# Feed-forward as one sequence with one ring of weight pieces: output parts of 6, 6, 6 chunks by seven products, 4 by eight, block sums on VectorE

## The reference, cut to what matters

```python
def swiglu(x, w_in, w_out):
    gate, up = jnp.split(x @ w_in, 2, axis=-1)
    return (jax.nn.silu(gate) * up) @ w_out

x = x + 0.5 * swiglu(rms_norm(x, ffn1_norm), ffn1_w_in, ffn1_w_out)
# mixers: attention, gated recurrence, short convolution
x = x + 0.5 * swiglu(rms_norm(x, ffn2_norm), ffn2_w_in, ffn2_w_out)
```

## Time and profile before

| | us |
|---|---|
| median of 3 runs | 2883.03 |
| lowest and highest run | 2880.31, 2888.37 |
| profiled execution, its own time | 2886.48 |
| span of the profiled execution | 2884.8 |
| TensorE matmuls busy | 2829.6 |
| VectorE busy | 1693.6 |
| ScalarE busy | 1112.6 |
| GpSimd busy | 312.8 |

### The profile page before, as it was taken

The page is one execution under the profiler, slowest core; times in us unless marked ns, Lnnn a source line. Parts: engine busy times, 40 slices in busy tenths (PEclk is TensorE's granted clock), DMA queues, the critical chain, the costliest instruction groups (busy, mean ns, idle before and its releaser), DMA issues.

```text
span 2884.8 us, 56179 instructions
## 1 busy us (share of the span) xinstructions
PE 2829.6 (98%) x21280; PEld 2764.3 (96%) x21280; DVE 1693.6 (59%) x2441; ACT 1112.6 (39%) x1669; POOL 312.8 (11%) x232
## 2 busy tenths in 40 slices
PE   7999999999999999999999999999999999999999
PEld 6999999899999999999999999998889999999998
DVE  4564756676655446656556565576666445575654
ACT  4332423555522333333333333335554223333324
POOL 1121201000000111111102021100000001030301
PEclk9999999999999999999999999999999999999999
DMA  3222223333222222222222223233332222222222
GB/s 121 73 88 87 88 74 99 90 96 87 82 80 87 89 85 70 95 73 97 80 76 87 88 73 103 74 89 90 90 107 71 87 80 97 74 81 95 73 88 91
DMA packets 299060, 249.22 MB, mean 86 GB/s; under 512 B 20643, under 2 KB 296307, under 8 KB 298919
## 3 DMA queue, kind: packets, MB, share of 16 engines
q1 hardware_dynamic: 296775, 242.44, 27.2%
q0 software_dynamic: 2144, 4.98, 0.5%
HBM read 240.04 MB, written 7.34 MB: 86 GB/s over the span
## 4 chain that ended last, share of the span: by engine, by line
PE 93%; DVE 3%; issue 1%; ACT 1%; DVEq 1%; DMA 0%; POOLq 0%; ACTq 0%; SPq 0%
PE ps L509 74%; PE ps L549 11%; PE ps L709 1%; PE ps L648 1%; PE ps L647 1%; PE ps L649 1%; PE ps L774 1%; PE ps L727 1%; PE ps L689 1%; DVE bl L1258 1%; DVE tmp L1223 1%; DVE wlo L1249 1%; PE ps L696 0%; PE ps L711 0%; DMA xin<-in_x_sample 0%
## 5 line engine op out<-in xcount | busy, mean ns | idle before, releaser
L509 PE MATMUL ps<-hh,whi 128*128 128x288 f32 x4480 | 965.3, 297 | 11.5 <-DVE wlo L1217 5.0
L509 PE MATMUL ps<-hl,whi 128*128 128x288 f32 x4480 | 959.3, 296 | 0.0
L509 PE MATMUL ps<-hh,wlo 128*128 128x288 f32 x4480 | 959.2, 296 | 0.0
L873 ACT ACTIVATE whi<-wraw 128x1024 fp32r<-128x1024 f32 (+1 forms) x388 | 403.9, 1042 | 1162.5 <-PE ps L509 1136.0
L509 PEld LDWEIGHTS ps<-hh,whi 128*128 128x128 f32 x4480 | 722.0, 189 | 14.2 <-DVE wlo L1217 5.9
L509 PEld LDWEIGHTS ps<-hh,wlo 128*128 128x128 f32 x4480 | 722.1, 189 | 0.0
L509 PEld LDWEIGHTS ps<-hl,whi 128*128 128x128 f32 x4480 | 721.9, 189 | 0.0
L1217 DVE TENSOR_TENSOR wlo<-wraw,whi 128x1024 fp32r<-128x1024 f32 (+1 forms) x388 | 467.0, 1204 | 374.4 <-ACT whi L873 373.6
L1266 DVE TENSOR_TENSOR tmp<-tmp,ps 128x576 f32<-128x576 f32 x128 | 96.6, 754 | 344.9 <-PE ps L509 344.5
L549 PE MATMUL ps<-bh,whi 128*128 128x288 f32 x896 | 266.8, 298 | 18.3 <-ACT tmp L956 12.8
L549 PE MATMUL ps<-bl,whi 128*128 128x288 f32 x896 | 264.3, 295 | 0.0
(11 more groups left out here) (333 smaller groups left out, 3549.9 us busy)
## 6 DMA issues: line engine op xcount, KB each, us to landing
wraw<-in_ffn_w_in SPq DMA_DIRECT2D x88, 1024.0 KB
wraw<-in_ffn_w_out SPq DMA_DIRECT2D x32, 1024.0 KB
wraw<-in_w_in SPq DMA_DIRECT2D x28, 1024.0 KB
wraw<-in_w_in SPq DMA_DIRECT2D x56, 512.0 KB
wraw<-in_ffn_w_out SPq DMA_DIRECT2D x16, 768.0 KB
wraw<-in_w_branch SPq DMA_DIRECT2D x24, 512.0 KB
wraw<-in_w_out SPq DMA_DIRECT2D x9, 1024.0 KB
kv<-in_cache_k SPq DMA_DIRECT2D x128, 64.0 KB, 1.8
```

The costliest lines, as they stand in the source:

```text
L509: last = pe.matmul(ps[slot][:, half, 0:HF], weights, rhs[:, k, half * HF:(half + 1) * HF], start=(start and c == 0 and n == 0), stop=(stop ...
L873: act.activation(split_tile(into, j, rowwise), raw_tile(slot, j, rowwise), ACT.Copy).then_inc(hi_ready, 1)
```

## The change

**One sequence.** A network is now one stage of 38 units, written out without loops: for each of 11 steps an up unit and then a gate unit (`whole`), four output units ahead of the gate unit of steps 3, 6 and 9, and four last output units. Parts one to three have 6 hidden chunks each, by seven products; the last part has 4, by eight. The gates and ups stay plain products.

**One ring.** Every tile, plain ones too, now passes through the ring of four as pieces: two of 512 columns for a gate or up tile, seven of 384 for an output unit, two of 256 for a last tile. After piece i, ScalarE and VectorE split piece i + 4.

**Sums on VectorE.** `weight_sums` leaves GpSimd. VectorE makes the sum for piece i + 6 after its split of piece i + 4, with a drain ahead of it, in three buffers in place of four.

**Moved.** The decay constants go from the preamble into the first network of each layer, behind the gate of step 4. `past_forgets` goes ahead of the last gate unit's load and waits for the third output part. The hidden blocks' last operations stand in the up unit that follows.

```diff
+STEPS = 11
+PART_STEPS = ((0, 1, 2), (3, 4, 5), (6, 7, 8), (9, 10))
+LAST = 9
+def ffn_units():
+    units = []
+    for s in range(STEPS):
+        units.append(("up", s, 0))
+        if s in (3, 6, 9):
+            units += [("out", s // 3 - 1, v) for v in range(4)]
+        units.append(("whole", s, 0))
+    return units + [("last", 3, v) for v in range(4)]
...
-        for pairs in (4, 4, 3):
-            s[name].append((Stage(plan, pairs, 2, 4), Stage(plan, 2, 2, 4), 2 * pairs))
+        s[name] = Stage(plan, 1, len(FFN_UNITS), 2 * len(FFN_UNITS))
...
-            bh = sb("bh", [P, 7, 4, HF], F32R, m)
-            wsum = sb("wsum", [P, 4, 4 * P], F32, m)
+                bh = sb("bh", [P, 7, 3, HF], F32R, m2)
+                wsum = sb("wsum", [P, 3, 4 * P], F32, m2)
...
             def ffn(name, L):
...
+                for n, (kind, s, v) in enumerate(FFN_UNITS):
+                    if kind == "up":
+                        load(S[name], n, L, 0, (w1, 0, KD, s * 256 + FFN, 256))
+                        if name == "ffn1" and s == STEPS - 1:
+                            past_forgets(L)
...
             def past_forgets(L):
-                norm = S["ffn1norm"]
-                wait_apart(sp, filled[norm.slot(0)], norm.turn(0, L) + 1)
+                st, k = S["ffn1"], 2 * FFN_UNITS.index(("out", 2, 3))
+                wait_apart(sp, filled[st.slot(k)], st.turn(k, L) + 1)
...
+            def ffn(name, nn, L):
+                st, f = S[name], nn // 2
+                root(S[name + "norm"], L)
+                i = 0
+                for n, (kind, s, v) in enumerate(FFN_UNITS):
+                    for m in range(7 if n in SEVEN_NO else 4):
+                        wait_done(act, st, f, i, L)
+                        if n in SEVEN_NO and m in (0, 1, 2, 4):
+                            parts(st, f, n, m, L)
+                        for j in BEHIND[i]:
+                            ring_split(st, f, j, L)
+                        if kind == "whole" and m % 2:
+                            if m == 3 and s < LAST:
+                                moving_first(f, s, s % 3, L)
...
+                            act.activation(buf, buf, ACT.Silu).then_inc(silu_ready, 1)
...
+            def weight_sum(st, f, i, L, first=None):
...
+                dve.drain()
...
+                dve.tensor_tensor(summed(n, m), x0, x1, op).then_inc(wsum_ready, 1)
...
+                        for j in BEHIND[i]:
+                            if j == 4:
+                                weight_sum(st, f, j + 1, L, first=i)
+                            ring_split(st, f, j, L)
+                            if j + 2 < len(ITEMS):
+                                weight_sum(st, f, j + 2, L)
...
+                        elif kind == "whole" and m == 3:
+                            if f == 0 and s == 4:
+                                dve.drain()
+                                decays()
+                            if s == STEPS - 1:
+                                odd_hidden(f, s, L)
...
-                for part in range(2):
-                    weight_sums(S["ffn1"][part][1], part_no(0, part), L)
```

More of the change, by code:

```diff
@@ L204, in build @@
             cmask = sb("cmask", [P, 2 * P], F32, m)
[L205 removed]
         with ExitStack() as m:
+            sb("over_th", [P, 8, 4 * HF], F32, m)
             yout = sb("yout", [P, 5, D], F32, m)
@@ new lines, in ring_ready, with seven @@
+            def ring_ready(st, f, i, L):
+                if COMB[i] is not None:
+                    pe.wait_ge(comb_lo, comb(L, f, i))
+                else:
+                    pe.wait_ge(lo_ready, st.unit(0, L) * 2 + (2 * ITEMS[i][0] + 2 + AHEAD))
+            def seven(st, f, n, i, L):
+                kind, s, v = FFN_UNITS[n]
+                first, second = ps[st.slot(2 * n)], ps[st.slot(2 * n + 1)]
+                a, b, c = first[:, 0, 0:HF], first[:, 1, 0:HF], second[:, 0, 0:HF]
+                half = chunks_of(n) // 2
+                for m, bank in enumerate((a, c, a, c, a, b, a)):
+                    ring_ready(st, f, i + m, L)
+                    if m < 2:
+                        wait_psum(st, 2 * n + m, L)
+                    if m in COPY_NO:
+                        pe.wait_ge(part_copied, copied(L, f, n, COPY_NO[m]))
+                    wh, wl = ring(whi, i + m), ring(wlo, i + m)
+                    x_ = MOVING[m]
+                    for kk in range(half):
+                        if v == 0:
+                            pe.wait_ge(mov_ready, blocks_ready(L, f, PART_STEPS[s][kk], MOVED[x_]))
+                        mov_h, mov_l = bh[:, x_, kk, :], bl[:, x_, kk, :]
+                        for t, (weights, moving) in enumerate(((wh, mov_h), (wh, mov_l), (wl, mov_h))):
+                            last = pe.matmul(bank, weights[:, kk, :], moving, start=(m in (0, 1, 5) and kk == 0 and t == 0),
+                                             stop=(m in (3, 5, 6) and kk == half - 1 and t == 2), skip_group_check=True)
+                    if m == 3:
+                        last.then_inc(filled[st.slot(2 * n + 1)], 1)
+                    elif m == 6:
+                        last.then_inc(filled[st.slot(2 * n)], 1)
+                    else:
+                        last.then_inc(product_done, 1)
@@ L970, in ffn, with buffers_free @@
[L970 to L990 removed]
+            def buffers_free(st, f, n, m, L):
+                kind, s, v = FFN_UNITS[n]
+                if kind == "out" and v == 0 and m == 0:
+                    act.wait_ge(mov_ready, blocks_ready(L, f, PART_STEPS[s][-1], 4))
@@ new lines, in parts @@
+            def parts(st, f, n, m, L):
+                kind, s, v = FFN_UNITS[n]
+                first, second = ps[st.slot(2 * n)], ps[st.slot(2 * n + 1)]
+                one, other = scratch(v)
+                places, scale = (one[:, 0:HF], other[:, HF:N], one[:, HF:N], None, other[:, 0:HF]), 0.5
+                buffers_free(st, f, n, m, L)
+                src = second[:, 0, 0:HF] if m == 1 else first[:, 0, 0:HF]
+                act.activation(places[m], src, ACT.Copy, scale=scale).then_inc(part_copied, 1)
@@ L1719, in _ @@
                     merge_step(i, False)
-                update(S["out"], L, 1.0, 16, L, 16)
+                update(S["out"], L, 16, L, 16)
                 dve.wait_ge(f_stored, L * 96 + 96)
@@ L1794, in _ @@
                 add_squares(L * 24 + 16)
-                for part in range(2):
-                    weight_sums(S["ffn2"][part][1], part_no(2, part), L)
                 add_squares(L * 24 + 24)
```

619 lines of the change are left out of this document (304 added, 315 removed).

## The result

The changed kernel takes 2901.1 us (median), the kernel before 2883.5 us beside it: a ratio of 1.0058, interval 1.0042 to 1.0074. One of its five runs took 11150.4 us, in the slow state, and is not in the ratio. The change makes the kernel slower by 0.58%, beyond the 0.3% that can be told apart, and 1 us above the upper end of the predicted range; the forecast was 2878. The profiled execution took 2901.01 us where the one before took 2886.48: 14.5 us more, where the sum of the prediction said 4.6 less. So 19.1 us have to be found.

What follows compares the result with a forecast made beforehand. TensorE, busy 98% of the span, was taken as the bound; -32.1 us removed and +27.5 added gave -4.6 net, so 2886.5 became 2882 profiled, 2878 as median, range 2858 to 2900.

Steps and rivals of the forecast that it cites:

- (a): Output parts by seven products, the last by eight: 948 products a network instead of 960, 48 fewer in all, -6.4 us.
- (b): The eight transitions where seven-product output units begin, two per network: TensorE's waits there all go, -21.2 us.
- The rival that the transitions stay: Waits move to the first unit of each output part, twelve parts cost 16 us, time 2894; chance 0.04.
- (c): At the four starts of a network TensorE goes on sooner, after one half split: -4.5 us, bounds -3 and -5.
- (d): Weight-block sums move from GpSimd to VectorE in the output units, so TensorE waits: +16 us, from 0 to 35.
- the loop: ScalarE and VectorE work in turn from one fourth sum to the next in output units: 8.73 us against TensorE's 8.45.
- binds harder: VectorE's in-order work between fourth sums at 36 output units costs up to 35 us, time 2897; chance 0.18.
- The Trainium skill's rule on drains: Next VectorE operation waits for an empty pipe: 9.4 us an output unit, about 38 us in all, result 2900.
- (e): At the gates' end, silu precedes the last hidden chunk; TensorE waits four times: +7 us, bounds 6 and 9.
- (f): TensorE waits once for every half piece, some 11 ns a wait: +3 us, bounds 0 and 4.
- (g): Past forgets' sixteen small loads on SyncE's queue hold the load behind them: +1.5 us for two layers, bounds 0 and 6.

Runs made afterwards that it cites:

- the second experiment: VectorE's drain and two additions of scratch to x moved from behind product five to behind product six, against the changed kernel: 2893.9 us, 1.0025 to the kernel before.
- the tenth experiment: On the kernel with the separate edits together, a network's last unit puts the addition to x and norm's cast ahead of the next stage's first split: 2867.2 us, 0.9929.

## Why the prediction was wrong

(a) **Right.** 48 fewer products; 3024 by seven, as the 1008 rows times three say.

(b) **Right, a little small.** The eight parts before lost 22.9 us beyond their products, where I took 21.2, and without the sums the new parts lose nothing. The rival that the transitions stay is out.

(c) **Right.** Behind the first tile the gates up to the first part now take 0.2 us more than their products, where they took 3.2, 0.7, 2.1 and 0.7 more: 6.0 against my 4.5.

(d) **Mechanism partly right, size too small**: 25.2 us, not 16. The forecast waits came where they were forecast, at the fourth product of the second to fourth unit of each part. By the starts each costs 0.47 us with the product behind it, 17 us in all for my 16; ScalarE's copy is ready there (248.07 in the second unit) just before VectorE's split (248.23). What I had left out are waits at the third product of the same units: 0.47, 0.11 and 0.19 us, together 9 us over the twelve parts. At the first of them, 246.69 above, TensorE waits for VectorE's split of the third piece, which stands behind the update of x:

```profile
245.64 0.45 DVE L1436 TENSOR_TENSOR x<-x,tmp 128x288 f32<-128x288 f32 x1
246.01 0.55 DVE L1344 TENSOR_TENSOR wlo<-wsum,whi 128x384 fp32r<-128x384 f32 x1
```

With the update late these waits are gone. Two terms of the loop were short too. The step from a split to the first sum takes 0.65 to 0.73 us, not 0.63: in the longer ones 0.17 is idle behind the drain. From ScalarE's split for the fourth sum to VectorE's last split it takes 2.05, not 1.88. That it is the loop alone fell with the second experiment: VectorE's own total, which I put at 8.66 and which by my prices is 8.50 without the drain that this edit saves, is 8.79 there. The point from which the "binds harder" rival decides was 9.1 us a unit; 9.03 was nearly there, and that rival had a chance of 0.18. The Trainium skill's rule on drains ("VectorE: DVE Perf Modes", section "The DRAIN you can't avoid"), by which I gave 9.4 us a unit and 2900 us, came near the measured time, but not for its reason. The section itself adds that a next operation that is not held starts earlier, and the trace agrees: undrained neighbours still start 0.47 us apart where each lasts 0.56. What a drain costs shows at the fourth sum: it starts 0.64 us after the split ahead of it with a drain between, 0.47 in the run without.

(e) **The wait right, the sentence behind it wrong.** Silu ahead of the last hidden chunk costs 1.6 us a network, 6.4 in all, against 7. The step that failed is the sentence with which I closed the term, "Behind it on VectorE stand only splits that TensorE needs later". That stage had not been stepped through. In it the pieces had become half pieces, the parts smaller and the chunks closer (3.2 us for 4.8), and the norm's chain had not; and each second split stood under GpSimd's addition. That is 1.5 us a network inside the stage, and it makes the last chunk late, whatever comes next: 3.1 us more before the transposes and 2.6 for their half clock, and 1.2 us at each of the two ways from the first feed-forward to the values. With the squares on VectorE the 1.5, the 1.2 and the half clock are gone, and the final wait is 1.8 us instead of 4.3. I had the contention in a row and used it only to say that it would go with the sums; GpSimd had one more job.

(f) **Wrong.** Half pieces with a wait each cost nothing: 576 plain products with a wait each 24 take 76.79 us, the last stage's 192 with a wait each 12 take 25.59 in the run with the tiles in turn, both 133.3 ns a product, and the parts without sums 133.0 ns with a wait each 9. The 0.9 ns in the old output stage belonged to that stage.

(g) **Right in kind and nearly in size.** 2.4 us for two layers, against 1.5.

**Open.** Why TensorE stands 2 to 4 us at the layer's turn before the third network, in every version with the new sequence. It stood there nearly as long in the kernel before:

```profile
1453.98 0.52 PE L509 MATMUL ps<-hh,whi 128*128 128x288 f32 x2 [1.80 <-issue]
```

So of the 2.1 us now only 0.3 can come from the change. The last stage's loss is not shown to be the cause either: without it the stop is longer, 3.9 us, and the tenth experiment moved the suspected work and not the stop. And which stop brings half clock: see below.

## What to carry to other kernels

When pieces are cut smaller, step through every stage that uses them, the shortest above all: a chain that ran once per piece now has less time for each, and each engine's order in it decides. Before a move off GpSimd is counted as the end of its contention, list what GpSimd still does, and what small VectorE operation stands in its way: the small one can pay the length of the large one, here 1.62 us for 0.41. And price a short wait of TensorE by the starts of the products around it, not by the list of waits, here 0.47 against 0.21.

## What the runs showed of the hardware

A stop of about 2 us sometimes brought TensorE's lower clock and sometimes not. At the third network's start, 2.1 us of waiting was followed by a first tile of 8.00 us in the changed kernel, and 2.3 us by one of 6.34 and 6.48 in the runs without the sums and with two drains fewer. The first tile of the program, behind the same 4.7 us in all versions of the new sequence, took from 7.85 to 9.14, and 7.81 in the kernel before. So some 1.3 to 1.5 us at such a place differ from one profile to the next without an edit that explains it, and a difference of that size there should not be put down to an edit.
